# Scratch with halo columns, moves inside SBUF and another order of groups in a gated-convolution encoder block

## The reference

```python
h = rmsnorm(x, norm_g) * (1.0 + scale[:, None, :]) + shift[:, None, :]
p = h @ w_in                                              # (B, L, IN_COLS)
a_in, a_b, a_c, a_z, b_v, b_g, b_z = jnp.split(p, SPLITS, axis=-1)
y_a = a_b * dwconv(a_c * a_in, conv_a_w) * jax.nn.silu(a_z)          # width 3
u = b_v * jax.nn.sigmoid(b_g)
u = dwconv(u, conv_b_w) + conv_b_b                                   # width 31
y_b = jax.nn.silu(head_layernorm(u, ln_g, ln_b)) * jax.nn.silu(b_z)
y = jnp.concatenate([y_a, y_b], axis=-1) @ w_out
return x + gate[:, None, :] * y                                      # then a final rmsnorm
```

## Time and profile before

| | |
|---|---|
| median of 3 runs | 2735.78 us (2735.37 to 2736.96) |
| the profiled execution | 2744.08 us |
| its span, slowest core (core 7) | 2742.4 us; the others 2722.3 to 2738.1 |
| busy share of the span | PE 85%, DVE 44%, ACT 42%, POOL 21% |
| mean granted TensorE clock, core 7 | 0.929 |
| DMA queue of SP and its share of 16 engines' span | 424.30 MB, 65.2% |
| HBM read, written | 288.04 MB, 117.56 MB |

### The profile page before, as it was taken

The page is one execution under the profiler, slowest core; times in us unless marked ns, Lnnn a source line. Parts: engine busy times, 40 slices in busy tenths (PEclk is TensorE's granted clock), DMA queues, the critical chain, the costliest instruction groups (busy, mean ns, idle before and its releaser), DMA issues.

```text
span 2742.4 us, 39503 instructions; the slowest of 8 cores (2722.3 to 2742.4 us)
## 1 busy us (share of the span) xinstructions
PE 2334.4 (85%) x11652; PEld 997.2 (36%) x11652; DVE 1193.9 (44%) x1911; ACT 1152.7 (42%) x1922; POOL 563.6 (21%) x574
## 2 busy tenths in 40 slices
PE   3866789989898998989898887988989879998786
PEld 0322334434333333434343333433434334343232
DVE  0233154453626345453635336253453624545156
ACT  1121535345263534536363442634436353453563
POOL 3011321211212121211212221123211232121311
PEclk8987899989999999999999899998999999999898
DMA  9966667574766757485766838577494785848865
GB/s 233 133 118 128 142 171 135 164 154 126 193 129 194 138 144 146 134 193 123 203 144 178 157 128 193 126 184 163 132 201 111 195 179 147 169 125 197 164 163 176
DMA packets 367900, 434.43 MB, mean 158 GB/s; under 512 B 162984, under 2 KB 301392, under 8 KB 367696
## 3 DMA queue, kind: packets, MB, share of 16 engines
q1 hardware_dynamic: 352960, 424.30, 65.2%
q0 software_dynamic: 7392, 7.34, 2.3%
q10 hardware_dynamic: 7344, 0.27, 0.4%
HBM read 288.04 MB, written 117.56 MB: 148 GB/s over the span
## 4 chain that ended last, share of the span: by engine, by line
PE 34%; DMA 24%; SPq 14%; DVE 9%; issue 8%; ACT 6%; POOL 3%; ACTq 1%; DVEq 0%; POOLq 0%
PE pb L455 22%; SPq L348 9%; PE pb L650 7%; DMA u_scratch<-u 6%; DMA xb<-x 4%; PE pb L566 3%; DVE tp L523 3%; DMA V<-u_scratch 3%; SPq L556 2%; DMA hT<-xs 2%; DMA yB<-y_scratch 2%; DMA g_scratch<-gst 2%; DMA y_scratch<-YP 2%; DMA xb<-w_out 2%; DVE xb L686 2%
## 5 line engine op out<-in xcount | busy, mean ns | idle before, releaser
L455 PE MATMUL pb<-hT,w_in_sb 128*128 128x512 bf16 x7168 | 1641.0, 388 | 111.6 <-DVE hT L354 74.5
L455 PEld LDWEIGHTS pb<-hT,w_in_sb 128*128 128x128 bf16 x7168 | 707.3, 99 | 1014.6 <-issue 221.6
L461 ACT ACTIVATE tp<-pb 128x512 f32<-128x512 f32 x384 | 226.4, 591 | 657.1 <-PE pb L455 457.8
L650 PE MATMUL pb<-w_out_sb,yA 128*128 128x512 bf16 x1024 | 286.2, 405 | 67.9 <-ACT gst L493 67.0
L650 PE MATMUL pb<-w_out_sb,yB 128*128 128x512 bf16 x1024 | 292.3, 403 | 47.6 <-DMA yB<-y_scratch 42.8
L464 DVE TENSOR_TENSOR t<-pb,tp 128x512 bf16<-128x512 f32 x128 | 88.1, 693 | 541.1 <-ACT tp L461 155.8
L676 ACT ACTIVATE tp<-xb 128x1024 bf16<-128x1024 f32 x128 | 135.3, 1057 | 371.6 <-DVE xb L661 260.7
L612 POOL TENSOR_TENSOR YP<-tp,YP 128x512 bf16<-128x512 f32 x128 | 146.2, 1163 | 672.5 <-ACT tp L610 672.5
L661 DVE TENSOR_TENSOR xb<-pb,xb 128x512 f32<-128x512 f32 x256 | 174.3, 688 | 187.9 <-PE pb L650 166.3
L321 ACT ACTIVATE tp<-xb 128x1024 bf16<-128x1024 f32 x128 | 134.6, 1053 | 258.4 <-DMA xb<-x 252.1
L523 DVE SCALAR_TENSOR_TENSOR tp<-t,caT_sb,tp 128x512 f32<-128x512 bf16 x256 | 217.0, 848 | 28.1 <-DVE tp L520 0.9
(11 more groups left out here) (65 smaller groups left out, 1234.6 us busy)
## 6 DMA issues: line engine op xcount, KB each, us to landing
xb<-x SPq DMA_DIRECT2D x256, 512.0 KB, 7.6
V<-u_scratch SPq DMA_DIRECT2D x512, 131.0 KB, 6.6
y<-xb SPq DMA_DIRECT2D x128, 512.0 KB, 3.5
xb<-w_out SPq DMA_DIRECT2D x40, 512.0 KB, 9.2
u_scratch<-u SPq DMA_DIRECT2D x128, 128.0 KB, 8.3
g_scratch<-gst SPq DMA_DIRECT2D x32, 512.0 KB, 4.4
YP<-g_scratch SPq DMA_DIRECT2D x16, 1024.0 KB, 6.3
y_scratch<-YP SPq DMA_DIRECT2D x32, 512.0 KB, 3.1
```

Source lines behind the costliest of these rows:

```text
L455: T.op("tensor", lambda e, bank=bank, kc=kc: e.matmul(bank[:], lhsT=w_in_sb[:, kc, col0:col0 + 128], rhs=hT2[q][:, kc, :], start=(kc == 0) ...
L461: T.op("scalar", lambda e: e.activation(out=t[:], in_=bank[:], func=func, scale=scale), reads=[bkey], writes=[tkey])
L650: T.op("tensor", lambda e, kc=kc, src=src: e.matmul(bank[:], lhsT=src, rhs=w_out_sb[:, kc, h * NT:(h + 1) * NT], start=(kc == 0), stop=(kc ...
```

## The change

- **Scratch of u.** Every window has its own block: per parity and group of 128 channels, 128 rows of 528 columns, with 8 halo columns on each side. The GLU columns of `w_in` are permuted on the host so that the 8 rows of one V partition follow each other. A V read is then 2 DMAs instead of 8, each to 64 partitions, with one run of 8440 bytes per partition; its source has dimensions 4 (shifts) x 16 x 4220. Each `u` write gets a second small DMA that puts its first and last 8 columns into the neighbours' halos. A V read waits for its own window's `u` and for two halo writes.
- **Gates and y.** `g_move` and `y_move` copy from SBUF to SBUF, 64 partitions at a time: 4 DMAs of 256 KB for the gates of a window and 8 of 128 KB for y, no DRAM between.
- **Order of groups.** Steps 0 to 3 are GLU of the even tile, 4 to 7 of the odd one; the even z gates (20, 21) stand ahead of `stage_d(p, 0)`; the odd z gates (22, 23) right behind it, the odd `ga` (24 to 27) last. V reads stand after steps 4, 6, 7 and 10, `conv2` after 7, 10, 13 and 16, `y_move` after 13 and 19.
- **Rows.** x rows of the even tile are loaded and scaled between steps 5 and 17, `a_transpose(0)` stands after step 21; `a_mod(w + 1, 0)` after steps 25 and 26, `a_mod(w, 1)` after steps 0 and 1 of the period that uses it.
- **Sequence starts.** `w_out` is loaded after steps 6 to 13 and scaled after 8 to 15.
- **Start.** All sixteen `w_ada` loads go to sixteen staging places (in `hT1`, `w_out_sb`, `WC`, `V`, `yB`, `YP`) without a wait; the odd rows' squares and transposes follow behind the `w_ada` matmuls; 4 of the 14 `w_in` loads stand ahead of them, the other 10 wait for the odd transposes. The gate's loads and matmuls lie in period 0's steps 4 to 19.
- **Last period.** It follows the same order, writes its y to other tiles, and spreads the last window's work over the two last `stage_d` of window 14.
- `XB` has 7 tiles, `u` a ring of 4.

The diff, cut to what the prediction speaks of:

```diff
-VW = NT + 12
+VW = NT + 2 * PAD
+VN = 8 * VW
...
-    LT = nwin * NT + PAD * (nseq + 1)
-    U_d = nc.dram_tensor("u_scratch", [2, 512, LT], BF16).ap()
-    GD_d = nc.dram_tensor("g_scratch", [4, 128, 2, NT], BF16).ap()
-    YD_d = nc.dram_tensor("y_scratch", [8, 128, NT], BF16).ap()
+    U_d = nc.dram_tensor("u_scratch", [nwin, 2, 4, 128, VW], BF16).ap()
...
-        u_sb = [sb("u%d" % i, [128, 4, NT], BF16) for i in range(2)]
+        UR = Ring("u", [sb("u%d" % i, [128, NT], BF16) for i in range(4)], T)
...
+        XB = Ring("xb", [sb("xb%d" % i, [128, D], F32) for i in range(7)], T)
...
+        for name, t_, n in (("hT1", hT2[1], 2), ("w_out", w_out_sb, 4), ("WC", WC, 2), ("V0", Vt[0], 2), ("V1", Vt[1], 2),
+                            ("yB", yB, 2), ("YP", YP, 2)):
+            dims = " ".join("abc"[:len(t_.shape) - 1])
+            f = t_[:].rearrange("p %s -> p (%s)" % (dims, dims)).bitcast(F32)
+            VK[name] = [("vs", len(stage) + i) for i in range(n)]
+            stage += [f[:, i * D:(i + 1) * D] for i in range(n)]
...
+        def u_pad(w, side):
+            c = 0 if side == 0 else PAD + NT
+            out = U_d[w].rearrange("a j (p g) t -> (a j p) g t", g=8)[:, :, c:c + PAD]
+            T.dma("scalar", lambda e: e.dma_start(out=out, in_=t1[0][:, 0, 0:8 * PAD].rearrange("p (g t) -> p g t", g=8)),
+                  reads=[("t1", 0, 0)], writes=[("Upad", w, side)], semkey=("up", w, side))
...
+                ub, ukey = UR.next()
+                T.op("vector", lambda e: e.scalar_tensor_tensor(out=ub[:], in0=t[:], scalar=1.0, in1=bank[:], op0=ALU.add, op1=ALU.mult),
+                     reads=[tkey, bkey], writes=[ukey])
+                T.dma("sync", lambda e: e.dma_start(out=u_rows(w, q, j, PAD, NT), in_=ub[:]),
+                      reads=[ukey], writes=[("U", q, j, w)], semkey=("uw",) + ukey)
...
+                if len(sides) == 2:
+                    dst = u_rows(w - 1, q, j, PAD + NT, PAD)
+                    dst = bass.AP(dst.tensor, dst.offset, [[VW, 128], [2 * 8 * 128 * VW - PAD - NT, 2], [1, PAD]])
+                    T.dma("sync", lambda e: e.dma_start(out=dst, in_=ub[:].rearrange("p (a t) -> p a t", t=PAD)[:, 0:NT // PAD:NT // PAD - 1, :]),
+                          reads=[ukey], writes=[("Uh", q, j, w)], semkey=("uh",) + ukey)
...
-        def g_write(q):
-            T.dma("sync", lambda e: e.dma_start(out=GD_d[:, :, q, :].rearrange("j p t -> p j t"), in_=gst[:]),
-                  reads=GSK, writes=[("GD", q)], semkey=("gw", q))
-
-        def g_read():
-            src = GD_d.rearrange("j (h x) q t -> (x q) (j h) t", h=2)
-            T.dma("sync", lambda e: e.dma_start(out=YP[:], in_=src),
-                  reads=[("GD", 0), ("GD", 1)], writes=[("yp", u) for u in range(8)], semkey="gr")
+        def g_move(q):
+            T._need("sync", T._deps("sync", [], VK["YP"]))
+            for h in range(2):
+                T.dma("sync", lambda e, h=h: e.dma_start(out=YP[q::2, h::2, :], in_=gst[64 * h:64 * h + 64, :, :]),
+                      reads=GSK, writes=[("yp", u, q) for u in range(h, 8, 2)], semkey=("gm", q, h))
 
...
-                deps = [("U", q, j, p)]
-                deps.append(("Upad", wseq[p], par) if wfirst[p] else ("U", q, j, p - 1))
-                deps.append(("Upad", wseq[p] + 1, par) if wlast[p] else ("U", q, j, p + 1))
-                for kap in range(4):
-                    r = 64 * par + 16 * kap
-                    c = ucol(p) - 8 + par + kap
-                    T.dma("sync", lambda e, par=par, r=r, c=c: e.dma_start(
-                        out=buf[r:r + 16, :, :], in_=U_d[par, j * 128:(j + 1) * 128, c:c + VW].rearrange("(g c) t -> c g t", c=16)),
-                        reads=deps, writes=[(key, 4 * par + kap)], semkey=("vl", key, par, kap))
+                deps = [("U", q, j, p), ("Upad", p, 0) if wfirst[p] else ("Uh", q, j, p - 1), ("Upad", p, 1) if wlast[p] else ("Uh", q, j, p + 1)]
+                src = U_d[p, par, j]
+                src = bass.AP(src.tensor, src.offset + par, [[1, 4], [VN, 16], [1, VN - 4]])
+                T.dma("sync", lambda e, par=par, src=src: e.dma_start(
+                    out=buf[64 * par:64 * par + 64, :, :].rearrange("p g t -> p (g t)")[:, 0:VN - 4], in_=src),
+                    reads=deps, writes=[(key, par)], semkey=("vl", key, par))
...
+        def y_move(hh):
+            T._need("sync", T._deps("sync", [], VK["yB"]))
+            yt, yk = out_y["yB"]
+            for q in range(2):
+                for h in range(2):
+                    us = (4 * hh + h, 4 * hh + h + 2)
+                    T.dma("sync", lambda e, q=q, h=h: e.dma_start(out=yt[64 * h:64 * h + 64, 2 * hh:2 * hh + 2, q, :],
+                                                                  in_=YP[q::2, 4 * hh + h:4 * hh + 4:2, :]),
+                          reads=[("yp", u, q) for u in us], writes=[(yk, 2 * hh, q, h), (yk, 2 * hh + 1, q, h)], semkey=("ym", hh, q, h))
...
-        def next_rows(post, w):
-            if w + 1 >= nwin:
-                return
-            n = w + 1
-            add(post, 17, lambda: a_load(n, 0, (0, 1)))
-            add(post, 20, lambda: a_load(n, 0, (2, 3)), lambda: a_half(0, 0))
-            add(post, 22, lambda: a_half(0, 1), lambda: a_load(n, 1, (0, 1)))
-            add(post, 23, lambda: a_transpose(0), lambda: a_load(n, 1, (2, 3)))
-            add(post, 24, lambda: a_square(1, 0), lambda: a_square(1, 1))
-            add(post, 25, lambda: a_scale(1, 0), lambda: a_square(1, 2), lambda: a_square(1, 3))
-            add(post, 26, lambda: a_scale(1, 1))
+        def rows_even(post, w):
+            if w + 1 < nwin:
+                n = w + 1
+                for i in range(4):
+                    add(post, 5 + 3 * i if w else 12 + i, lambda i=i: a_load(n, 0, (i,)))
+                    add(post, 8 + 3 * i if w else 17 + i, lambda i=i: a_square(0, i))
+                add(post, 11 if w else 18, lambda: a_scale(0, 0))
+                add(post, 17 if w else 20, lambda: a_scale(0, 1))
+                add(post, 21, lambda: a_transpose(0))
+
+        def rows_odd(post, w):
+            if w + 1 < nwin:
+                n = w + 1
+                add(post, 22, lambda: a_load(n, 1, (2, 3)))
+                add(post, 24, lambda: a_half(1, 0))
+                add(post, 25, lambda: a_half(1, 1), lambda: a_mod(n, 0, range(4)))
+                add(post, 26, lambda: a_mod(n, 0, range(4, 8)))
+                add(post, 27, lambda: a_transpose(1))
 
...
-            late = 2 if p == 0 else 0
-            add(post, 1 + (3 if late else 0), lambda: vread(p, 0))
-            add(post, 3 + late, lambda: vread(p, 1))
-            for j, h in enumerate((5 + late, 8 + late, 11 + late, 14 + late)):
+            add(post, 4, lambda: vread(p, 0))
+            add(post, 6, lambda: vread(p, 1))
+            for j, h in enumerate((7, 10, 13, 16)):
...
+            add(post, 13, lambda: y_move(0))
+            add(post, 19, lambda: y_move(1))
...
+            add(post, 0, lambda: a_mod(w, 1, range(4)))
+            add(post, 1, lambda: a_mod(w, 1, range(4, 8)))
+            for j in range(4):
+                add(post, j, lambda: d_finish() if fin else None)
+                add(post, (3, 5, 6, 7)[j], lambda j=j: conv_a(p, 1, j))
...
+                add(post, 6, lambda: wout_gate(wseq[p]))
...
-                    add(post, 2 + kc, lambda kc=kc: wout_load(kc))
-                    add(post, 3 + kc, lambda kc=kc: wout_mul(kc))
+                    add(post, 6 + kc, lambda kc=kc: wout_load(kc))
+                    add(post, 8 + kc, lambda kc=kc: wout_mul(kc))
...
-        def glu_pairs(w):
-            e, o = pairs("glu", w, 0, 0), pairs("glu", w, 1, 0)
-            if w == 1:
-                return e + [(4 + j, o[j][1]) for j in range(4)]
-            return [(2 * j + q, (e, o)[q][j][1]) for j in range(4) for q in range(2)]
+        def sixteen(w):
+            return pairs("glu", w, 0, 0) + pairs("glu", w, 1, 4) + pairs("a1", w, 0, 8) + pairs("a1", w, 1, 12)
...
-            head(w, mid, post)
-            add(post, 15, lambda: d_load(p, 0, (0, 1)))
-            add(post, 16, lambda: d_load(p, 0, (2, 3)))
-            next_rows(post, w)
-            for j in range(4):
-                add(post, 20 + j, lambda j=j: conv_a(w, 0, j))
-            add(post, 20, lambda: d_finish() if fin else None)
-            add(post, 21, lambda: d_finish() if fin else None, lambda: g_write(0))
-            add(post, 25, lambda: d_load(p, 1, (0, 1)))
+            head(w, post)
+            rows_even(post, w)
+            add(post, 17, lambda: d_load(p, 0, (0, 1)))
+            add(post, 18, lambda: d_load(p, 0, (2, 3)))
+            add(post, 21, lambda: g_move(0))
+            steps(sixteen(w) + pairs("a2", w, 0, 16) + zpairs(0, 20), mid, post)
+            stage_d(p, 0, hooks={5: lambda: a_load(w + 1, 1, (0, 1))})
+            mid, post = {}, {}
+            finish_one()
+            conv_a(w, 0, 0)
+            for j in range(1, 4):
```

(22 more changed lines are left out.)

224 lines of the change are left out of this document (99 added, 125 removed).

## The result

The changed kernel takes 2876.3 us (median of 4 runs), the one before 2735.6 us in the same comparison: ratio 1.0502, 95% interval 1.0458 to 1.0546. It is 5% slower. The forecast was 2595 us, faster with 0.87; the time lies far outside the range of 2440 to 2700. In what follows kernels are compared by their ratio to the kernel before, which ran beside each of them on the same chip and took 2705 to 2737 us itself; some runs were disturbed on some cores and up to 13% longer, and the ratios leave these out.

The account below looks back on a forecast made before the run. PE, busy 85% of the span, was taken as the bound. From 2744.1 us, 240 came off and 29, 20, 40 and 10 were added: 2603 us profiled, 2595 us as a median; range 2440 to 2700.

Parts of the forecast that it names:

- Term 6: First V read of a window, at today's 125 GB/s: 15 waits of 5.5 us, +29 us, half clock +20.
- the other three reads have room: A window's second to fourth V reads: convolutions come every 13.3 us against 11 a read, so no waits.
- Rival B: V reads chain the period: 26.4 + 4d + 69 us, d a read's data time; slower from 15.5 us; 12%.
- Rival A: The V read is fast, up to 370 GB/s: all V waits and their half clock go, median 2455 us; 22%.
- Terms 1 to 5: Gains of 240 us: hT waits 65, gst waits 67, yB waits 30, gate 26, start 7, half clock 45.
- Terms 1, 2, 4 and 5: PE's waits for hT (65 us) and gst (67), gate (26) and start (7), half clock behind hT and gst (45).
- late squares: Squares late for their x rows delay tp copies of the last ga steps: 0 to 2 us a period, +10 us.
- Term 3: Moves of gates and y inside SBUF, one hop instead of two: 30 of 42.8 us of yB waits go.
- Term 4: Gate matmuls moved into period 0, -25.9 us; sixteen w_ada loads back to back, 7 us off the start.
- Term 7: Periods that load w_out: x scaling shares POOL's steps, loads stand behind V reads; +8 us in each of 5, 40.
- Rival C: w_out periods clog on POOL, SP and ACT: 25 us in each of 5 periods instead of 8, 2680 us; 13%.
- What would show it: Signs in the profile: hT and gst under 10 us each, V waits of 4 to 8 us at first conv_b only.

Follow-up runs that it names:

- e1_spread: The changed kernel with V reads' partitions in order (channel, shift), slowest source dimension 16 instead of 4, conv weights' rows permuted to match; 2420.8 us, ratio 0.8904.
- e7_split8: The changed kernel with each V read as eight DMAs of 16 partitions, one per half and shift, partition order kept; ratio 0.9183, about 2498 us.
- e3_spread_pads: e1_spread with each zero-halo write issued in its own window's period instead of all ten in period 0; ratio 0.8738.
- e5_k8: e1_spread with each half V read as two DMAs of 8 channels x 4 shifts, slowest source dimension 8; ratio 0.9162, about 2492 us.

## Why the prediction was wrong

**Term 6, the V read, failed**, and in one place: "at the 125 GB/s of today's read". The rest of the count was right: the first read is issued 768.62 - 747.37 = 21.2 us into the period (forecast 21.6), and PE stops for it at 27.8 (forecast 28). I took today's rate since scratch, tile and bytes stayed, though the DMA's shape did not: eight DMAs with 16 channels outermost had become two with the 4 shifts outermost. Measured are 77 GB/s, by which the data need 14.0 us instead of 8.6, and 19.9 us from issue to use instead of 11.0, with the x load and `u` writes that share the engines. The first conv_b waited 13.3 us and not 5.5. The next sentence fell with it, "the other three reads have room": the second read is issued when the halo write behind the first has landed, as the prediction says, but that is now at 788.81, 20 us after the first, and against a cadence of 13.3 it is late by 6.5 us. The third and fourth are issued long before their use (the fourth 845.13 - 813.32 = 31.8 us) and are in time. V waits are 268 us where 82 were forecast.

**The number of engines was what I had left out of the sum.** The windows show a DMA share of 0.25 with 4 outermost, 0.54 with 8 and about 1 with 16. The Trainium skill ("DMA: Bandwidth & Descriptors", section on why a DMA increments its semaphore by 16) says that a transfer uses the largest number of engines up to 16 that divides the slowest dimension on both sides; by this rule 4, 8 and 16 engines work here, and the trace agrees. The estimate from it was 92 GB/s and 11.7 us; the measured 77 GB/s are lower still, and the 33 us that I gave it, outside the sum, were far too few, since I priced only the first wait. By the measured difference between e1_spread and the changed kernel the choice of outermost dimension is worth 0.160, 436 us, of which V waits are 237.

**Rival B, slower, came nearest**, at 12%, and half by luck. With the 14.0 us that the data would need alone, its formula gives 26.4 + 4 x 14.0 + 69 = 151 us, no longer than today's period; with what the read really took less the fixed part, 19.9 - 2.4 = 17.5 us, it gives 165.4, and 166.6 were measured. Its point of decision, 15.5 us, lies between the two. But the four reads do not stand one behind the other, as the formula has it: the second does, the third is issued 3 us after it, and PE's stops of 13 and 6 us and the waits behind them (sq, tp and t at conv_b) make up the rest. Rival A fell as a forecast, yet with the engines spread its number was near: 2455 forecast, 2421 measured in e1_spread. Its thought that the partitions reached count fits what e7_split8 showed, though the 104 GB/s that it set beside our 125 is a fifth lower, no close agreement.

**Terms 1 to 5** were 240 us. With the read's shape mended they can be weighed, but only net of what the order costs. Terms 1, 2, 4 and 5 (order and start) were 210 us, less 49 for term 6, 40 for term 7 and 10 for late squares: 111 net. Measured are 0.035 to 0.038, about 100 us. The net was near, its parts were not: hT and gst did go (of hT's 29.8 us in e1_spread 25.1 are one wait at the start), but part of hT's wait (68.2 to 30.4 us) belongs to the moves, the halo writes took 45 us that I had costed at nothing, and term 7 gave where it should have cost. **Term 3** came to 103 to 111 us instead of 30: I counted the yB waits and not the other waits (hT in the old order, V in the new one) and the clock behind them. **Term 4** had the wrong sign at the start: scale and shift were ready 16 us earlier, but the even transposes stood behind all sixteen w_ada loads, and w_in matmuls began at 70.98 us instead of 65; the 45 us of the halo writes in period 0 (e3_spread_pads) come on top.

**Term 7** had the wrong sign: the w_out period costs 178.1 - 157.2 = 21 us over the plain one ahead of it, 28 before; I forecast 36. In e1_spread the same two periods, counted from one window's first conv_b to the next (1249.4, 1390.0 and 1533.2 us), take 140.6 and 143.2 us: 3 us for w_out. The slow read carries most of the 21. Rival C did not happen.

**What would show it.** hT and gst went as written, apart from the start; V was the longest line, but with waits at the second read, which the prediction had named as the sign that it is wrong; the other sign, a new wait over 50 us, came too (tp, 52.6 us, at the halo writes). Plain periods were 157 to 167 us, not 143 to 149; in e1_spread they are 139 to 143.

Left open: how much of e1_spread's lead over e5_k8 is engines and how much SP's two more issues a read and the smaller DMAs; what limits a DMA of 16 partitions to 125 to 135 GB/s; and how the gain of the moves divides between SP's time and the traffic.

## What to carry to other kernels

When a DMA's access pattern changes, its rate is not that of the old one, however alike bytes, tensor and tile are: look at which dimension is slowest on each side, and put one there that all engines can share. A transfer with a duplicated (overlapping) read has that choice free: permute the partitions and the weights with them. Keep many partitions in one DMA as well: here all engines were busy at 135 GB/s with 16 of them, and moved about 250 with 64. Look also at what stands behind a slow transfer: a small write there can hold back the next one. And price a hop through DRAM by what the issuing engine's wait for the first landing holds up, not by the wait of the last consumer alone.

## What the hardware showed

Of ten DMAs of 1024 pieces of 16 bytes each, 0.16 MB in all, six held their issuing engine for 58.5 us and a seventh for 14.4, in the stretch in which w_in is loaded; one at a time they took 0.52 us each to issue, and spreading them was worth 45 us of the program. Eight transposes behind twenty-four loads on one queue took 42.6 us from the first issue to the last, where four took 9.6 in the steady state. Four DMA engines moved 70 to 91 GB/s between them in the windows shown of the two kernels with 4 outermost, on a share of 0.24 to 0.26, a level so even that the share alone names the number of engines. A share near 1 is no sign of a good rate, though: it stood for 125 and 135 GB/s with 16 partitions a DMA, for some 250 with 64, and for 370 in loads of x with 128.
